# Rotating queries and keys beside their projection, and transposing the latents' tiles between the attention heads

## The chip, the cores and the metric

The kernel runs on one core of one Trainium2 chip. The metric is the device time of one execution in microseconds; the time before is the median of three runs. All arithmetic is in 32-bit floats.

## The reference, cut to what matters

The whole program is a two-layer network with a third block behind it. The change touches only the first mixer of the first layer. It has 512 tokens, 256 of a context and 256 latents, in four tiles of 128 (tiles 0 and 1 are the context, 2 and 3 the latents). What is computed there:

```python
q_m, k_m, v_m, o_m, g_m, q_a, k_a, v_a = _split(h @ w_in, AB_WIDTHS)
outs = [_directional(_mlstm_scan, mc + gc[d], ml + gl[d], init, d == 1) for d in range(2)]
a_lat = _window_attention(_rope(ql, cos, sin), _rope(kl, cos, sin), vl, kc, vc, sink)
a_ctx = _context_attention(qc, kc, vc, sink)
cat = [head_norm(m) * sigmoid(o_m), a];  y = cat @ w_out

def _rope(x, cos, sin):
    x1, x2 = x[..., 0::2], x[..., 1::2]
    return stack([x1 * cos - x2 * sin, x1 * sin + x2 * cos], -1)
```

Attention has 8 query heads of width 64, and 2 key heads, each shared by 4 query heads. Context queries see the 256 context keys; latent queries see these and the latents within 128 positions, so up to 512. Context queries and keys have no positions; the kernel rotates them by an angle of zero (cosine 1, sine 0), so that all four tiles go one way.

## The kernel before, in words

The program is a row of stages. Each stage has its own semaphores and its own program per engine, and ends with a barrier: all engines finish, GpSimd clears the stage's semaphores one by one, and the next stage starts on all of them. So a stage lasts as long as its slowest engine, and nothing of the next one can start earlier, except the weight tiles: `Weights` holds two slots of 2 MB, and whoever frees a slot has SyncE (SP) load the tile that comes after next, also across stages.

The stages around the change:

- **ab_qkv** (`stage_linear`) projects to queries (512 columns), keys (128) and values (128): 768 columns, as one tile of 512 columns and one of 256. For each, TensorE runs 32 products (4 token tiles times 8 slices of the depth), and the four banks are then copied to `qkv`. When a linear stage has no side work (`both`), ScalarE and VectorE copy two banks each; when it has (`side`), ScalarE copies all four (line 215) and VectorE runs the side's parts.
- **mlstm** (`stage_mlstm`), 8 units of matrix products, exponentials and products on VectorE, with one tile of "modulation" in each unit. Its result goes to `hm`.
- **attn** (`stage_attention`). VectorE first rotates one token tile (lines 1266 to 1279) into single buffers `qr` and `kr`; TensorE turns them by five 128x128 transposes (lines 1175, 1176) into the PSUM tile `ps_t`; ScalarE copies them out to `qt` and `kt` (1227, 1228); and so on for four tiles. Then come 32 units, 8 heads for each token tile: 16 context units, numbers 0 to 15, and 16 latent units, 16 to 31. In a step of its loop, for unit u, TensorE multiplies the scores of unit u+2 (1186), transposes the exponentials of unit u+1 (1196) and multiplies the output of unit u (1216). VectorE masks the scores and takes their maximum (1293 to 1300) and scales the output (1312 to 1315); ScalarE takes the exponentials (1242, 1243) and copies the transposed ones (1256).
- Amid these units run four tiles of **modulation** (`Modulation`, lines 413 to 464): a product of a 2 MB weight tile with the conditions (16 short matmul records, 413), a copy to SBUF (430), a product that adds up the parts (422), a sum with the bias (438, 443), and a DMA that stores the row (464). `share` says in which unit a tile runs: tile i in unit i * 32 // 4, that is in units 0, 8, 16 and 24. When a tile's product is done, SP loads the weight tile after next into its slot (113); at the end of the stage SP waits until all rows are stored (469). The modulation's two PSUM banks are those of `ps_t`.
- **ab_norm** (`stage_head_norm`) reads `hm` and writes the first half of `cat`; attention has written the second half. Then `cat` is transposed and projected.

## Time and profile before

| | us |
|---|---|
| median of 3 runs | 3768.81 (3768.76 to 3774.37) |
| the profiled execution, its own time | 3774.25 |
| its span, first to last instruction | 3772.4 |
| TensorE, busy in the span | 3024.5 (80%) |
| VectorE | 1991.3 (53%) |
| ScalarE | 791.2 (21%) |
| GpSimd | 879.9 (23%) |

The two long stretches in the middle of the program are the expert layers, which wait for DMA; the mixer of the change lies at about 60 to 475 us. A line of the timeline gives the start, the duration, the engine, the line of the kernel, what is written and read, how often, and in square brackets how long the engine had been idle and what ended that. PEld is TensorE's loading of weights. The granted clock is 1.00 at 2.4 GHz and 0.50 at 1.2 GHz.

### The profile page before, as it was taken

The numbers are of one execution on the slowest core, as the hardware profiler recorded it, in microseconds if no ns is written. First come the engines' busy times: TensorE is split into PE (matmuls) and PEld (weight loads), VectorE is DVE, ScalarE is ACT, GpSimd is POOL, SyncE is SP. The second block draws the span as 40 slices with busy tenths as digits, with TensorE's granted clock in tenths as the row PEclk, the third lists the DMA queues.
The fourth block names the chain that finished last, engine by engine and source line by source line (L and its number), as shares of the span: only waits on it lengthen the run. The fifth ranks groups of instructions, "written<-read, shape, count | busy, mean of one in ns | idle before, by whom it ended". The sixth has DMA issues, their size and how long they took to land. (4 is left out here: it accounts for less than half of the span.)

```text
span 3772.4 us, 28092 instructions
## 1 busy us (share of the span) xinstructions
PE 3024.5 (80%) x8564; PEld 1486.2 (39%) x8564; DVE 1991.3 (53%) x5057; ACT 791.2 (21%) x2002; POOL 879.9 (23%) x772
## 2 busy tenths in 40 slices
PE   7987788888888888777488667878877597897898
PEld 3444443333333333322243334333332355453663
DVE  1135567777777777776610756767776323223100
ACT  0112312222222222222101312222222130122000
POOL 0000014444444444444100003444444000000000
PEclk9996899999999999999788689999999898898999
DMA  5143229999999999999612247999999343323333
GB/s 195 57 157 112 90 114 427 427 427 427 427 427 423 423 421 417 426 416 427 262 45 91 90 157 322 427 427 427 427 427 427 142 139 116 112 105 130 112 134 122
DMA packets 238156, 1026.04 MB, mean 272 GB/s; under 512 B 41399, under 2 KB 46007, under 8 KB 137639
## 3 DMA queue, kind: packets, MB, share of 16 engines
q0 software_dynamic: 110592, 805.36, 50.8%
q1 hardware_dynamic: 126984, 217.63, 16.5%
q8 instruction: 66, 1.08, 0.1%
q10 hardware_dynamic: 432, 1.31, 0.1%
q14 instruction: 82, 0.66, 0.0%
HBM read 1023.10 MB, written 1.13 MB: 272 GB/s over the span
## 5 line engine op out<-in xcount | busy, mean ns | idle before, releaser
L1528 PE MATMUL l_peer_experts_acc<-l_peer_experts_ring,l_peer_experts_diag 128*128 128x512 f32 x1840 | 860.9, 610 | 217.3 <-ACT l_peer_experts_diag L1567 216.8
L1688 DVE SCALAR_TENSOR_TENSOR l_peer_experts_ring<-l_peer_experts_ring,h_tiles 128x1024 f32<-128x1024 f32 x460 | 563.6, 1225 | 287.4 <-DMA l_peer_experts_ring<-in_expert_rows,l_peer_experts_picks 283.9
L1528 PE MATMUL l_peer_experts_acc<-weight_slots,l_peer_experts_diag 128*128 128x512 f32 x1232 | 581.2, 614 | 150.9 <-ACT l_peer_experts_diag L1567 150.6
L1470 POOL DMA_INDIRECT weight_slots<-in_expert_rows,l_peer_experts_picks x308 | 348.1, 1130 | 1431.1 <-DVE l_peer_experts_picks L1647 1009.0
L1470 POOL DMA_INDIRECT l_peer_experts_ring<-in_expert_rows,l_peer_experts_picks x460 | 531.7, 1156 | 611.5 <-PE l_peer_experts_acc L1528 538.1
L1528 PEld LDWEIGHTS l_peer_experts_acc<-l_peer_experts_ring,l_peer_experts_diag 128*128 128x128 f32 x1840 | 337.4, 192 | 710.9 <-issue 397.3
L1688 DVE SCALAR_TENSOR_TENSOR weight_slots<-weight_slots,h_tiles 128x1024 f32<-128x1024 f32 x308 | 377.4, 1225 | 190.8 <-DMA weight_slots<-in_expert_rows,l_peer_experts_picks 188.3
L1528 PEld LDWEIGHTS l_peer_experts_acc<-weight_slots,l_peer_experts_diag 128*128 128x128 f32 x1232 | 227.9, 194 | 481.7 <-issue 274.7
L1560 ACT ACTIVATE l_peer_experts_gel<-l_peer_experts_dots 128x2 f32<-128x2 f32 x384 | 78.2, 204 | 1207.6 <-DVE l_peer_experts_ring L1688 727.1
L1567 ACT ACTIVATE l_peer_experts_diag<-const_ident,l_peer_experts_wgt 128x128 f32<-128x128 f32 x768 | 266.4, 394 | 225.8 <-DVE l_peer_experts_wgt L1664 209.8
L1495 PE MATMUL l_peer_experts_queries<-h_t,l_query_weights 128*128 128x512 f32 (+3 forms) x576 | 182.0, 461 | 3.9 <-PEq L61 3.9
L1495 PEld LDWEIGHTS l_peer_experts_queries<-h_t,l_query_weights 128*128 128x128 f32 x576 | 106.2, 201 | 76.0 <-issue 67.3
L191 PE MATMUL b_mlp_acc<-weight_slots,b_up 128*128 128x512 f32 x256 | 111.5, 599 | 3.9 <-DVEq L280 3.9
L191 PE MATMUL b_mlp_acc<-b_h_t,weight_slots 128*128 128x256 f32 x512 | 110.8, 379 | 2.5 <-ACTq L266 2.5
L191 PEld LDWEIGHTS b_mlp_acc<-b_h_t,weight_slots 128*128 128x128 f32 x512 | 97.2, 190 | 16.0 <-ACTq L266 2.9
L191 PE MATMUL b_g_acc<-weight_slots,b_h_t 128*128 128x512 f32 x192 | 88.3, 614 | 10.4 <-ACTq L266 10.4
L1664 DVE TENSOR_TENSOR l_peer_experts_wgt<-l_peer_experts_gel,l_peer_experts_scratch 128x2 f32<-128x2 f32 x384 | 60.1, 157 | 52.6 <-ACT l_peer_experts_gel L1560 23.1
L191 PEld LDWEIGHTS b_mlp_acc<-weight_slots,b_up 128*128 128x128 f32 x256 | 49.2, 193 | 65.8 <-issue 65.8
L288 DVE TENSOR_TENSOR b_up<-b_up x8 | 9.8, 1225 | 108.6 <-ACT b_up L215 108.6
L213 DVE COPY b_down<-b_mlp_acc 128x512 f32<-128x512 f32 x2 | 1.4, 692 | 111.9 <-PE b_mlp_acc L191 111.9
L191 PE MATMUL b_xbc_acc<-b_h_t,weight_slots 128*128 128x256 f32 x256 | 58.0, 387 | 2.1 <-ACTq L266 2.1
L191 PE MATMUL b_za_acc<-weight_slots,b_h_t 128*128 128x512 f32 x128 | 57.4, 606 | 2.5 <-ACTq L266 2.5
(464 smaller groups left out, 3367.1 us busy)
## 6 DMA issues: line engine op xcount, KB each, us to landing
weight_slots<-in_w_mod SPq DMA_DIRECT2D x24, 2048.0 KB, 7.8
weight_slots<-in_w_in SPq DMA_DIRECT2D x20, 2048.0 KB, 7.7
l_query_weights<-query_weights SPq DMA_DIRECT2D x16, 1024.0 KB, 9.0
weight_slots<-in_w_mlp_up SPq DMA_DIRECT2D x8, 2048.0 KB, 7.8
weight_slots<-in_w_mlp_down SPq DMA_DIRECT2D x8, 2048.0 KB, 7.7
weight_slots<-in_gla_w_in SPq DMA_DIRECT2D x6, 2048.0 KB, 8.4
weight_slots<-in_ab_w_in SPq DMA_DIRECT2D x5, 2048.0 KB, 8.8
l_ln_rows<-mod_rows SPq DMA_DIRECT2D x16, 512.0 KB, 9.5
```

The source lines that it names most:

```text
L191: last = nc.tensor.matmul(acc[0:rows, half, bank, col:col + cols], lhs, rhs, start=(b == 0 and k == 0), stop=(b == kb - 1 and k == KC - 1))
L213: ins = nc.vector.tensor_copy(dst, src)
L288: nc.vector.tensor_tensor(dst, dst, dst, ALU.mult)
L1470: pool.indirect_dma_start(rows(b, k, None), None, uv, bass.IndirectOffsetOnAxis(ap=picks[:, b % 4, k:k + 1], axis=0)).then_inc(landing(b, ...
L1495: ins = nc.tensor.matmul(q_ps[:, n % 2, 0:hi - lo], wq_slots[:, visit % 2, k, half * P:(half + 1) * P], h_t[:, k, g * n_tok + lo:g * n_tok ...
L1528: ins = nc.tensor.matmul(acc[:, b % 2, c * BANK:(c + 1) * BANK], diag[:, k % DIAGS, :], row[:, c * BANK:(c + 1) * BANK], start=(k == 0), s ...
L1560: nc.scalar.activation(gel[:, b % 2, two], dots[:, b % 2, two], ACT.Gelu).then_inc(gelu_done, 1)
L1567: scaled = nc.scalar.activation(diag[:, k % DIAGS, :], ident, ACT.Copy, scale=wgt[:, b % 2, k:k + 1])
L1664: nc.vector.tensor_tensor(wgt[:, step % 2, two], gel[:, step % 2, two], share[:, step % 2, two], ALU.mult).then_inc(w_ready, 1)
L1688: nc.vector.scalar_tensor_tensor(row, row, 1.0, h[:, tile_of(b), :], ALU.mult, ALU.mult, accum_out=dots[:, b % 2, k:k + 1]).then_inc(dotte ...
```

## The change

Four edits belong together.

1. The rotation leaves attention. `rotation_parts` is handed to ab_qkv as its side work: VectorE rotates the queries of all four tiles once the first column tile (512 columns, the queries) is copied out, and the keys of all four tiles, in one go, once the second is. `qr` and `kr` now hold all four tiles, and to make room `hm` is no longer a tensor of its own: it is the first half of `cat`, and ab_norm works in place.
2. Because ab_qkv now has side work, ScalarE copies all four banks, and VectorE none.
3. In attention only token tiles 0 and 1 are transposed ahead of the units. Tile 2 is transposed in unit 1, tile 3 in unit 3 (TensorE: `turn_in`; ScalarE: `copy_in`).
4. The modulation's tiles run in units 5, 13, 21 and 29 (`shift=5`), since they share the PSUM banks of the transposes.

```diff
+        st.emptied = act_out
         parts = side(st) if side else []
...
-        return [i for i in range(self.tiles) if i * units // self.tiles == u]
+        return [i for i in range(self.tiles) if i * units // self.tiles + self.shift == u]
...
+def rotation_parts(nc, st, qkv, cos, sin, qr, kr):
...
+    def queries(dve):
+        nonlocal links
+        link = Link(dve, chain)
+        dve.wait_ge(st.emptied, 3)
+        for m in range(TT):
+            x = qkv[:, m, 0:A_Q].rearrange("p (h r two) -> p h r two", two=2, r=32)
+            c, s = (w[:, m, :].unsqueeze(1).to_broadcast([P, H_A, 32]) for w in (cos, sin))
+            p1, p2, p3, p4 = products(link, x[:, :, :, 0], x[:, :, :, 1], c, s, None)
...
+    def keys(dve):
+        link = Link(dve, chain, links)
+        dve.wait_ge(st.emptied, 4)
...
+    return [{"vector": queries}, {"vector": keys}]
...
-        mod = Modulation(nc, st, weights, "mod1_first", *mod_args, 0, [ps_t[:, i, :] for i in range(2)])
+        mod = Modulation(nc, st, weights, "mod1_first", *mod_args, 0, [ps_t[:, i, :] for i in range(2)], shift=5)
...
+                turn_in(0)
+                turn_in(1)
+
+                pe.wait_ge(copied, 2)
...
                 for u, (m, kv, j) in enumerate(units):
+                    if u in (1, 3):
+                        turn_in(2 + u // 2)
+                    if u == 5:
+                        pe.wait_ge(copied, TT)
...
+                copy_in(0)
+                copy_in(1)
                 exponentials(0)
                 for u, (m, kv, j) in enumerate(units):
                     b, n = u % 2, keys(m)
+                    if u in (1, 3):
+                        copy_in(2 + u // 2)
                     if u + 1 < len(units):
                         exponentials(u + 1)
...
-        hm = sb("ab_hm", [P, TT, M_W])
+        hm = cat[:, :, 0:M_W]
...
-            stage_linear(nc, "ab_qkv", weights, h_t, tiles, qkv)
+            qr = sb("ab_qr", [P, TT, GROUP, H_KV, DH_A])
+            kr = sb("ab_kr", [P, TT, H_KV, DH_A])
+            stage_linear(nc, "ab_qkv", weights, h_t, tiles, qkv,
+                         side=lambda st: rotation_parts(nc, st, qkv, consts["cos"], consts["sin"], qr, kr))
```

On ScalarE, the copies at the end of ab_qkv, before:

```order
L215 ACTIVATE ab_qkv<-ab_qkv_acc 128x512 [waits ab_qkv_mm_done]
L215 ACTIVATE ab_qkv<-ab_qkv_acc 128x512
L215 ACTIVATE ab_qkv<-ab_qkv_acc 128x256 [waits ab_qkv_mm_done]
L215 ACTIVATE ab_qkv<-ab_qkv_acc 128x256
```

and of the change (ScalarE's copies; then VectorE's first tile of queries and, behind the fourth tile, the keys, where `ab_qkv_rot` are the four buffers of products):

```order
L216 ACTIVATE ab_qkv<-ab_qkv_acc 128x512 [waits ab_qkv_mm_done]
L216 ACTIVATE ab_qkv<-ab_qkv_acc 128x512 x3
L216 ACTIVATE ab_qkv<-ab_qkv_acc 128x256 [waits ab_qkv_mm_done]
L216 ACTIVATE ab_qkv<-ab_qkv_acc 128x256 x3
...
L1137 TENSOR_TENSOR ab_qkv_rot<-ab_qkv,const_cos 128x256 [waits ab_qkv_act_out]
L1138 TENSOR_TENSOR ab_qkv_rot<-ab_qkv,const_sin 128x256
L1139 TENSOR_TENSOR ab_qkv_rot<-ab_qkv,const_sin 128x256
L1140 TENSOR_TENSOR ab_qkv_rot<-ab_qkv,const_cos 128x256
L1155 TENSOR_TENSOR ab_qr<-ab_qkv_rot 128x4x32 [waits ab_qkv_rot_chain]
...
L1167 TENSOR_TENSOR ab_kr<-ab_qkv_rot 128x256 x2
```

VectorE's four copies are gone from this stage, ScalarE has four more, and VectorE has 38 rotation instructions in their place: 32 for the queries and 6 for the keys.

On TensorE, the first units of attention, before (`attn_turn` is the PSUM tile `ps_t`; L413 is a modulation tile):

```order
L1186 MATMUL attn_scores<-attn_kt,attn_qt 128x256 [waits attn_masked]
L1196 MATMUL attn_p_turn<-const_ident,attn_p 128x128 [waits attn_exped]
L1196 MATMUL attn_p_turn<-const_ident,attn_p 128x128
L413 MATMUL attn_turn<-weight_slots,silu_c 32x512 [waits weights_loaded0]
L413 MATMUL attn_turn<-weight_slots,silu_c 32x512 x7
L1216 MATMUL attn_out<-ab_qkv,attn_pt 128x64 [waits attn_p_copied]
L1216 MATMUL attn_out<-ab_qkv,attn_pt 128x64
L422 MATMUL attn_turn<-attn_mod_parts,const_add_up 2x512 [waits attn_mod_parted]
```

and of the change, from the score of unit 2 on:

```order
L1228 MATMUL attn_scores<-attn_kt,attn_qt 128x256 [waits attn_masked]
L1238 MATMUL attn_p_turn<-const_ident,attn_p 128x128 [waits attn_exped]
L1238 MATMUL attn_p_turn<-const_ident,attn_p 128x128
L1262 MATMUL attn_out<-ab_qkv,attn_pt 128x64 [waits attn_p_copied]
L1262 MATMUL attn_out<-ab_qkv,attn_pt 128x64
L1214 MATMUL attn_turn<-const_ident,ab_qr 128x128 [waits attn_copied]
L1214 MATMUL attn_turn<-const_ident,ab_qr 128x128 x3
L1215 MATMUL attn_turn<-const_ident,ab_kr 128x128
L1228 MATMUL attn_scores<-attn_kt,attn_qt 128x256 [waits attn_masked]
L1238 MATMUL attn_p_turn<-const_ident,attn_p 128x128 [waits attn_p_copied,attn_exped]
```

The modulation tile has left unit 0, and unit 1 begins with the five transposes of tile 2.

On TensorE, the end of attention in the change, where unit 29 now holds a modulation tile:

```order
L414 MATMUL attn_turn<-weight_slots,silu_c 32x512 [waits attn_mod_taken,weights_loaded1]
L414 MATMUL attn_turn<-weight_slots,silu_c 32x512 x7
L1262 MATMUL attn_out<-ab_qkv,attn_pt 128x64 [waits attn_out_taken,attn_p_copied]
L1262 MATMUL attn_out<-ab_qkv,attn_pt 128x64 x3
L423 MATMUL attn_turn<-attn_mod_parts,const_add_up 2x512 [waits attn_mod_parted]
L1238 MATMUL attn_p_turn<-const_ident,attn_p 128x128 [waits attn_p_copied,attn_exped]
```

Only two units come behind it, where seven came behind the last tile before.

## Rows read from the trace of the kernel before

**Rows 1.** Busy time, clock and DMA in the attention stage (columns in the first line).

```profile
core 0: us, PE busy (x) PEld busy (x) DVE busy (x) ACT busy (x) POOL busy (x), PEclk, DMA share, GB/s
312.60:434.90 122.30, 101.42 (x444) 58.38 (x444) 81.41 (x274) 44.14 (x136) 0.00 (x0) 0.74 0.20 70
```

**Rows 2.** Timeline: copies out of PSUM in ab_o and ab_qkv, then mlstm's start.

```profile
170.74 2.06 ACT L215 ACTIVATE ab_o<-ab_o_acc 128x512 f32<-128x512 f32 x4 [1.75 <-PE ab_o_acc L191]
...
218.38 0.66 ACT L215 ACTIVATE ab_qkv<-ab_qkv_acc 128x256 f32<-128x256 f32 x2 [12.73 <-PE ab_qkv_acc L191]
218.38 0.76 DVE L213 COPY ab_qkv<-ab_qkv_acc 128x256 f32<-128x256 f32 x2 [12.52 <-PE ab_qkv_acc L191]
...
219.91 1.09 PE L1029 MATMUL mlstm_m_bcast<-ab_m_rows,const_sel 4*128 4x512 f32 x2 [1.57 <-PEq L61]
```

**Rows 3.** Timeline: rotation of the first of four tiles in attention, its transposes.

```profile
312.66 0.49 DVE L1266 TENSOR_TENSOR attn_rot<-ab_qkv,const_cos 128x320 f32<-128x320 f32 x1 [3.17 <-PEq L61]
...
313.88 0.48 DVE L1269 TENSOR_TENSOR attn_rot<-ab_qkv,const_cos 128x320 f32<-128x320 f32 x1
314.39 0.49 DVE L1277 TENSOR_TENSOR attn_qr<-attn_rot 128x128 f32<-128x128 f32 x2
...
315.80 0.47 PE L1175 MATMUL attn_turn<-const_ident,attn_qr 128*128 128x128 f32 x1 [8.22 <-DVEq L1280]
```

**Rows 4.** Timeline: the last tile's transposes, and the first scores.

```profile
325.32 1.12 PE L1175 MATMUL attn_turn<-const_ident,attn_qr 128*128 128x128 f32 x4 [1.84 <-DVEq L1280]
...
327.65 2.07 PE L1186 MATMUL attn_scores<-attn_kt,attn_qt 64*128 64x256 f32 x4 [0.99 <-ACT attn_kt L1228]
```

**Rows 5.** Timeline: the score products that open units 0, 4, 8 and 9.

```profile
331.79 1.22 PE L1186 MATMUL attn_scores<-attn_kt,attn_qt 64*128 64x256 f32 x2
...
344.57 1.22 PE L1186 MATMUL attn_scores<-attn_kt,attn_qt 64*128 64x256 f32 x2
...
354.62 1.22 PE L1186 MATMUL attn_scores<-attn_kt,attn_qt 64*128 64x256 f32 x2
...
361.79 0.70 PE L1186 MATMUL attn_scores<-attn_kt,attn_qt 64*128 64x256 f32 x2
```

**Rows 6.** Timeline: the same products where they open units 12, 15, 16, 17, 19.

```profile
367.84 1.22 PE L1186 MATMUL attn_scores<-attn_kt,attn_qt 64*128 64x256 f32 x2
...
376.23 2.07 PE L1186 MATMUL attn_scores<-attn_kt,attn_qt 64*128 64x512 f32 x2
380.03 2.07 PE L1186 MATMUL attn_scores<-attn_kt,attn_qt 64*128 64x512 f32 x2
...
388.91 1.12 PE L1186 MATMUL attn_scores<-attn_kt,attn_qt 64*128 64x512 f32 x2
...
394.52 1.12 PE L1186 MATMUL attn_scores<-attn_kt,attn_qt 64*128 64x512 f32 x2
```

**Rows 7.** Timeline: modulation in unit 24, the stage's last result, the next stage.

```profile
410.43 1.92 PE L413 MATMUL attn_turn<-weight_slots,silu_c 128*32 128x512 f32 x16
...
432.47 0.28 DVE L1315 TENSOR_SCALAR h_tiles<-attn_out,attn_small 128x64 f32<-128x64 f32 x1 [0.63 <-PE attn_out L1216]
434.91 0.40 ACTq L1334 DMA_DIRECT2D ab_norm_rows<-in_ab_norm_w  x1
```

**Rows 8.** DMA issues between 200 and 440 us, KB and us to landing.

```profile
weight_slots<-in_w_mod SPq DMA_DIRECT2D x12, 2048.0 KB, 7.8
...
attn_sink<-in_ab_sink SPq DMA_DIRECT2D x1, 4.0 KB, 2.5
```

**Rows 9.** Windows: ab_qkv's first products; then units 10 to 13 (columns: rows 1).

```profile
175.00:176.00 1.00, 0.87 (x2) 0.63 (x3) 0.00 (x0) 0.00 (x0) 0.00 (x0) 0.81 0.20 66
...
179.00:180.00 1.00, 1.00 (x4) 0.48 (x3) 0.00 (x0) 0.00 (x0) 0.00 (x0) 0.98 0.00 0
...
364.00:368.00 4.00, 3.02 (x15) 2.31 (x15) 3.47 (x15) 2.33 (x10) 0.00 (x0) 0.85 0.81 313
368.00:372.00 4.00, 4.00 (x13) 2.58 (x14) 2.40 (x9) 1.76 (x7) 0.00 (x0) 0.50 0.00 0
```

More of the change, by code:

```diff
@@ L1124, in stage_mlstm, with products @@
     mod.done()
-def stage_attention(nc, qkv, cos, sin, bars, sink, ident, cat, weights, mod_args):
-    heads = H_A + H_KV
+def rotation_parts(nc, st, qkv, cos, sin, qr, kr):
+    t1, t2, t3, t4 = (st.sb(f"rot{i}", [P, H_A, 32]) for i in range(4))
+    chain, rotated = st.sem("rot_chain"), st.sem("rotated")
+    links = 0
+    def products(link, x1, x2, c, s, shape):
+        parts = [t[:, :, :] if shape is None else t[:, :, :].rearrange("p (m h) r -> p m h r", h=shape) for t in (t1, t2, t3, t4)]
+        nc.vector.tensor_tensor(parts[0], x1, c, ALU.mult)
+        nc.vector.tensor_tensor(parts[1], x2, s, ALU.mult)
+        nc.vector.tensor_tensor(parts[2], x1, s, ALU.mult)
+        link(nc.vector.tensor_tensor(parts[3], x2, c, ALU.mult))
+        return parts
+    def queries(dve):
[6 more added lines that the diff above has]
+            p1, p2, p3, p4 = products(link, x[:, :, :, 0], x[:, :, :, 1], c, s, None)
+            for a, b, op, which in ((p1, p2, ALU.subtract, 0), (p3, p4, ALU.add, 1)):
+                for kv in range(H_KV):
+                    hs = slice(kv * GROUP, (kv + 1) * GROUP)
+                    o = qr[:, m, :, kv, :].rearrange("p j (r two) -> p j r two", two=2)[:, :, :, which]
+                    last = nc.vector.tensor_tensor(o, a[:, hs, :], b[:, hs, :], op)
+                link(last)
+        links = link.n
+    def keys(dve):
+        link = Link(dve, chain, links)
+        dve.wait_ge(st.emptied, 4)
+        x = qkv[:, :, A_Q:A_Q + A_KV].rearrange("p m (h r two) -> p m h r two", two=2, r=32)
+        c, s = (w[:, :, :].unsqueeze(2).to_broadcast([P, TT, H_KV, 32]) for w in (cos, sin))
+        p1, p2, p3, p4 = products(link, x[:, :, :, :, 0], x[:, :, :, :, 1], c, s, H_KV)
+        for a, b, op, which in ((p1, p2, ALU.subtract, 0), (p3, p4, ALU.add, 1)):
+            o = kr[:, :, :, :].rearrange("p m h (r two) -> p m h r two", two=2)[:, :, :, :, which]
+            link(nc.vector.tensor_tensor(o, a, b, op))
+    return [{"vector": queries}, {"vector": keys}]
@@ L1135, in stage_attention @@
+def stage_attention(nc, qkv, qr, kr, bars, sink, ident, cat, weights, mod_args):
     scale = DH_A ** -0.5
     with stage(nc, "attn") as st:
-        qr = st.sb("qr", [P, GROUP, H_KV, DH_A])
-        kr = st.sb("kr", [P, H_KV, DH_A])
-        t1, t2, t3, t4 = (st.sb(f"rot{i}", [P, heads, 32]) for i in range(4))
         qt = st.sb("qt", [P, GROUP, TOK])
@@ L1168, in _, with turn_in @@
             def _(pe):
-                for m in range(TT):
-                    pe.wait_ge(rotated, m + 1)
+                def turn_in(m):
                     if m:
@@ L1174, in _ @@
                     for j in range(GROUP):
[L1175 to L1178 removed]
+                        nc.tensor.transpose(ps_t[:, 0, j * P:(j + 1) * P], qr[:, m, j, :, :].rearrange("p a b -> p (a b)"), ident)
+                    nc.tensor.transpose(ps_t[:, 1, 0:P], kr[:, m, :, :].rearrange("p a b -> p (a b)"), ident).then_inc(turned, 1)
+                turn_in(0)
+                turn_in(1)
+                pe.wait_ge(copied, 2)
                 def score(u):
@@ L1223, in _, with copy_in @@
                 link = Link(act, achain)
-                for m in range(TT):
+                def copy_in(m):
                     act.wait_ge(turned, m + 1)
```

32 lines of the change are left out of this document (5 added, 27 removed).

## The prediction

> **What bounds the kernel now.** I read the busy time by stage first, then the timeline around each edit, then the windows for the granted clock, then SyncE's DMAs. The stages are separated by barriers and the change touches three of them, so the question is what each of the three gains or loses; the expert layers behind them see nothing of it. Attention takes 122.3 us, at a mean granted clock of 0.74 [rows 1]: TensorE is at 1.2 GHz for much of it. Its first 15 us are no attention at all: VectorE rotates, TensorE turns, ScalarE copies. One tile costs 3.17 us: the fourth tile's transposes begin at 325.32, the first's at 315.80, and a third of the difference is 3.17 [rows 3, 4]. TensorE idles there. The first scores begin at 327.65 [rows 4], 15.0 us after the stage's start. After that the units run. At the low clock TensorE sets the pace of the context units: four of them take 354.62 - 344.57 = 10.05, so 2.51 each [rows 5]. For some units after a modulation tile the clock is high: units 9 to 11 take 367.84 - 361.79 = 6.05, about 2.0 each [rows 5, 6]. A context unit with a modulation tile at the low clock takes 361.79 - 354.62 = 7.17 [rows 5].
>
> **1. The projection gets longer.** The keys' tile now has four copies on ScalarE instead of two. Two take 0.66 [rows 2], four about 1.3; four copies of 512 columns took 2.06 in the stage before [rows 2]. VectorE's two ended at 219.14 (218.38 + 0.76), the four will end at about 219.65: +0.5. Then the keys are rotated with nothing to cover them. A product of 320 columns starts 0.41 after the last ((313.88 - 312.66) / 3) and the chained one needs 0.51 [rows 3]; for 256 columns I scale the part beyond the 0.22 of a short one and get 0.34 and 0.44. So 3 x 0.34 + 0.44 = 1.46, and two chained results of 256 columns, 2 x 0.44: 2.34 in all, plus 0.1 to be released. Two more semaphores to clear I put at 0.15. **Sum +3.1** (2.5 to 4).
> The queries cost nothing: per tile 1.46, and four results of 128 columns, which start 0.21 apart [rows 3] and are chained twice, 1.06. Four tiles take 10.1 and start when ScalarE has copied the first column tile, at about 206.8; they end at about 217, while TensorE multiplies until 218.4. The cover has 1.4 us to spare, and 2.7 before the keys want VectorE. Were it gone, each us over would be a us on the stage.
>
> **2. mlstm starts with TensorE colder.** TensorE's gap between the two stages was 1.5 us, 218.4 to 219.91 [rows 2], and becomes 4.6. A gap of 4.4 with little in it precedes ab_qkv (ab_o's products end at 170.7), and there the clock falls to half 0.6 us into the new stage and comes back after 3.4 us [rows 9]. Half speed for 3.4 us costs 1.7 of TensorE's time, and mlstm begins with a row of products that everything waits for. **+1.6** (0 if the clock holds, to 2.5). In mlstm's units the clock dips anyway; I expect no more there. That `hm` lies in `cat` changes addresses, no instruction: 0.
>
> **3. Attention's start gets shorter.** Two tiles are turned instead of four, and no rotation is waited for. From a tile's first transpose to the next thing TensorE can do is 327.65 - 325.32 = 2.33 [rows 4], so scores begin 4.66 after the start instead of 15.0: **-10.3**.
>
> **4. Two tiles are turned amid the units.** This is not only 1.4 us of transposes. In unit 1 ScalarE's next instructions are the copies, ahead of the exponentials that TensorE's next transposes wait for; so a unit is the turn (1.4), the copies (0.9), the exponentials (0.9) and then the rest as before. Against a low-clock unit I count 2.1 more: 4.6 instead of 2.5, twice. At least the transposes' 1.4, at most the whole 2.33 plus a release, 2.6.
>
> **5. The modulation moves, and the clock with it.** From the first scores to unit 0 it is 331.79 - 327.65 = 4.1, as before. Then, with rows 5 and 6 for each kind of unit: unit 0 2.5, units 1 to 4 4.6 + 2.5 + 4.6 + 2.5, unit 5 with modulation 7.2, units 6 to 8 6.05, units 9 to 12 10.0, unit 13 with modulation 7.2. Units 14 to 16 now run right behind a modulation tile, so at the high clock. Two latent units at the high clock take 394.52 - 388.91 = 5.6 [rows 6]; the first behind a modulation tile is short; I put the three at 7.2 (6 to 8.4). Unit 17 then begins 58.5 after the first scores; before it was 388.91 - 327.65 = 61.3, with units 15 at 3.8 and 16, with its modulation, at 8.9 [rows 6]. So **-2.8**, with the turns of part 4 already in it. Unit 17 loses its catch-up: +0.3. Modulation 24 becomes 21, at the same clock: 0.
>
> **6. The last modulation comes late.** Behind unit 24 seven units followed, behind 29 only two. The product takes 1.92 [rows 7] and part of it hides in the last units' waits for ScalarE; walking the last three units through with their durations, the last result comes 1.05 later, at 433.8 in the old time. But SP must see the row stored before the stage can end. In the same old time the product is done at 429.05, a 2 MB weight load is issued there, and the store at about 432.3. A load of that size takes 7.8 to land [rows 8]; if the little store lands with it, that is 436.85. From a stage's last work to the next stage's first instruction it is 0.77 at least (219.91 - 219.14 [rows 2]) and 2.16 here (434.91 less the last result's end at 432.75 [rows 7]), so the next stage would start at 437.6 to 439.0; the engines alone would give 433.8 + 2.16 = 436.0. The wait costs 1.6 to 3.0 more, or 0 to 1.0 if the store takes the 2.5 of a small transfer [rows 8]. I take 2.3, because the store is issued in the middle of the load. The Trainium skill, in DMA: Bandwidth & Descriptors, section Queues, rings and completion order, says that the semaphore write of a transfer lands only after every earlier write from that DMA engine. By that rule the sum is the one I make; by the other price it would be 1.8 us lower. **+1.05 and +2.3.**
>
> **The sum.** Attention: -10.3 - 2.8 + 0.3 + 1.05 + 2.3 = -9.5. With +3.1 and +1.6: **-4.8 us**. The profiled execution took 3774.25 (its span 3772.4), which is at the upper end of the three runs; the sum is a difference, and I take it from the median: 3768.8 - 4.8 = 3764.0. That is 0.13% of the time, and about 0.2%, 7.5 us, is what a measurement of this kernel can tell from no change.
>
> **The rivals.**
> A. **The clock drops as the latents begin.** Units 10 to 13 show it falling some 7 us behind a modulation tile, from 0.85 to 0.50 [rows 9]. What holds it before is the modulation in unit 16, in the thick of the latents. If it falls at unit 16 and stays low to the modulation in 21, five units run at the low clock. Such a unit is the 3.8 of unit 15 [rows 6] plus 0.9 for its longer output, 4.7 instead of 2.8: 5 x 1.9 = 9.5, and 1.0 for modulation 21 at the low clock. -4.8 + 10.5 = +5.7, **3774.5, slower than before**. It decides at unit 16: low clock there and this rival is right. Against it: latent units keep TensorE busier than context units, and once high, the clock stayed: the score product takes 2.07 at 380.03 and 1.12 at 388.91 and 394.52 [rows 6], and modulation 24, 22 us further on, still goes through in 1.92 [rows 7].
> B. **TensorE warms up at once.** With no rotation to wait for, its first 15 us are denser. If the high clock comes by unit 0, the plain units 0, 2, 4 save 0.5 each, the units with turns 1.2 each, modulation 5 some 1.2: -5.1, **3758.9**. The Trainium skill, in TensorE: Matmul & The Clock Gate, Part 1, says that the throttled state is the default and that activity releases it. What speaks against it is that units 4 to 8 kept TensorE at work without a gap for 12 us and the clock stayed low until the modulation's products: the unit at 354.62 still opens with a product of 1.22, that at 361.79 with one of 0.70 [rows 5].
> C. **The turns cost less or the projection's end more than I think**, without a new mechanism: mlstm's start may be warm (-1.6), the store may be quick (-1.8), the keys or the turns may take a microsecond more. This is the forecast's own range, 3760 to 3768.5. That the queries' rotation isn't covered, so that the change doesn't do what it says, would need VectorE 14% slower than its rows show; I give that 3 in 100, inside C.
>
> **How the numbers follow.** Forecast and C 0.74, A 0.13, B 0.13. The range takes in B and C, and most of A, whose price is an upper one, since a later clock rise would cut it: 3758.5 to 3773. Faster by over 7.5 us: most of B, and the low tail of the forecast, 0.2. Slower by over 7.5 us: A with the projection's upper bound, 0.05. Within: 0.75.
>
> **What would show it.** In the changed profile: ab_qkv's last rotation ends at about 222.1 and mlstm starts near 223; VectorE idle between queries and keys; mlstm's first products at clock 0.5; scores 4.7 us after attention's start; units 1 and 3 of 4.6; units 14 to 20 at clock 1.0; SP waiting at attention's end for a row's store. The prediction is wrong if the three stages together, from 174.8 to ab_norm's start, change by anything but -9 to 0 us, or if the stages behind change at all.

## The result, and the profile after

The changed kernel takes 3782.51 us (median of 15 runs), the kernel before, run beside it, 3773.61 us (15 runs). The ratio is 1.0024, with a 95% interval of 1.0017 to 1.0031: **8.9 us slower**. The forecast was 4.8 us faster. The profiled execution took 3777.12 (span 3775.3) against 3774.25.

The stages touched, by the first instruction of each in the two traces (each figure is rounded by itself):

| us | before | after | difference | forecast |
|---|---|---|---|---|
| ab_qkv | 44.8 | 48.6 | +3.8 | +3.1 |
| mlstm | 92.8 | 95.4 | +2.7 | +1.6 |
| attention | 122.3 | 125.0 | +2.7 | -9.5 |
| ab_norm and ab_turn | 22.8 | 22.0 | -0.7 | 0 |
| sum, to ab_out's first product | 282.6 | 291.1 | +8.5 | -4.8 |

The sum is close to the 8.9 us between the medians. What lies behind these stages can't be read that finely from one trace each: from ab_out's first product to the end it is 3314.7 us before and 3310.3 in the changed kernel, and between 3306.5 and 3319.7 in the fourteen traces of this study, none of which edits anything there. With 1.2 us less ahead of these stages, that is why the two profiled executions are only 2.9 us apart. By the prediction's own sign of being wrong, the three stages together changed by +9.2 us, outside -9 to 0. Windows of the changed kernel over the same stages, TensorE alone (columns in the first line):

```profile
core 0: us, PE busy (x), PEclk, DMA share, GB/s
174.00:222.58 48.58, 43.74 (x129) 0.95 0.20 70
222.58:318.00 95.42, 76.24 (x352) 0.86 0.52 186
318.00:442.95 124.95, 110.16 (x444) 0.69 0.19 68
```

Attention runs the same 444 matrix records as before, but they take 110.2 us where they took 101.4, and the mean granted clock is 0.69, not 0.74 [rows 1]. That is the first thing to see: the stage lost its rotation and yet TensorE is busy for longer.

**The projection's end and mlstm's start.** Timeline of the changed kernel:

```profile
217.78 1.21 ACT L216 ACTIVATE ab_qkv<-ab_qkv_acc 128x256 f32<-128x256 f32 x4 [11.75 <-PE ab_qkv_acc L192]
219.10 0.43 DVE L1137 TENSOR_TENSOR ab_qkv_rot<-ab_qkv,const_cos 128x256 f32<-128x256 f32 x1 [2.97 <-ACT ab_qkv L216]
...
220.56 0.89 DVE L1167 TENSOR_TENSOR ab_kr<-ab_qkv_rot 128x256 f32<-128x256 f32 x2
...
222.58 1.73 PE L1030 MATMUL mlstm_m_bcast<-ab_m_rows,const_sel 4*128 4x512 f32 x2 [4.84 <-PEq L61]
224.24 6.41 PE L1021 MATMUL mlstm_scores<-y_tiles 128*128 128x512 f32 x8
```

Four copies in 1.21 us, the keys rotated from 219.10 to 221.45, the next stage 1.1 us later. VectorE was idle for 2.97 before the keys, so the queries' rotation was covered. TensorE was idle for 4.84 us where it had been 1.57 [rows 2], and its first row of score products takes 6.41 us.

**Attention.** The first scores begin at 322.64, 4.6 us after the stage's start. The turn of tile 2, in unit 1:

```profile
329.15 1.06 PE L1214 MATMUL attn_turn<-const_ident,ab_qr 128*128 128x128 f32 x4
330.00 0.42 PE L1215 MATMUL attn_turn<-const_ident,ab_kr 128*128 128x128 f32 x1
...
332.09 0.69 PE L1238 MATMUL attn_p_turn<-const_ident,attn_p 128*128 128x128 f32 x2 [0.52 <-ACT attn_p L1290]
...
333.45 1.22 PE L1228 MATMUL attn_scores<-attn_kt,attn_qt 64*128 64x256 f32 x2
```

The unit takes 4.3 us. So far it goes as forecast. Now the same engine as the latents begin (units 15 to 20), then the modulation in unit 21:

```profile
374.03 1.12 PE L1228 MATMUL attn_scores<-attn_kt,attn_qt 64*128 64x512 f32 x2
376.31 0.98 PE L1238 MATMUL attn_p_turn<-const_ident,attn_p 128*128 128x128 f32 x4 [1.16 <-ACT attn_p L1290]
377.08 0.95 PE L1262 MATMUL attn_out<-ab_qkv,attn_pt 128*128 128x64 f32 x4
377.96 2.07 PE L1228 MATMUL attn_scores<-attn_kt,attn_qt 64*128 64x512 f32 x2
...
396.56 2.07 PE L1228 MATMUL attn_scores<-attn_kt,attn_qt 64*128 64x512 f32 x2
...
401.21 2.07 PE L1228 MATMUL attn_scores<-attn_kt,attn_qt 64*128 64x512 f32 x2
...
404.26 3.37 PE L414 MATMUL attn_turn<-weight_slots,silu_c 128*32 128x512 f32 x16
```

The score product doubles from 1.12 to 2.07 between 374.03 and 377.96 and stays there. From 377.96 to 401.21 there are five units, 16 to 20, of 4.65 us; before, two latent units at the high clock took 5.6 together [rows 6]. The granted clock in windows of the changed kernel:

```profile
222.00:223.00 1.00, 0.42 (x1) 0.95 1.04 408
223.00:224.00 1.00, 1.00 (x2) 0.50 1.06 412
...
370.00:376.00 6.00, 4.91 (x23) 1.00 0.75 259
377.00:407.00 30.00, 30.00 (x98) 0.50 0.01 5
407.00:441.00 34.00, 28.39 (x168) 1.00 0.35 125
```

The low level, 1.2 GHz, holds from 376.5 to 407.2. In the kernel before it ended at 387.2, behind the modulation tile in unit 16. A TensorE busy for 30.00 of 30.00 us is no sign of health here: it is busy because it is slow.

**Attention's end.** Timeline of the changed kernel, then SyncE's waits between 430 and 444 us (us in all, times, the longest):

```profile
433.05 0.39 SPq L113 DMA_DIRECT2D weight_slots<-in_ab_w_out  x1
...
436.16 0.23 SPq L465 DMA_DIRECT2D mod_rows<-attn_mod_rows  x1
...
437.46 0.28 DVE L1345 TENSOR_SCALAR h_tiles<-attn_out,attn_small 128x64 f32<-128x64 f32 x1 [0.40 <-PE attn_out L1262]
442.94 0.40 ACTq L1364 DMA_DIRECT2D ab_norm_rows<-in_ab_norm_w  x1
```

```profile
SPq L470 <- DMA mod_rows<-attn_mod_rows: 4.3, 1, 4.3
```

From the last result's end (437.74) to the next stage it is 5.2 us, where it was 2.16 [rows 7]: 3.0 more. The store of 4 KB, issued at 436.16, is waited for until 440.7; the last of the 2 MB load issued ahead of it lands at 440.9.

So two suspects are large (the clock in the latents, the colder mlstm) and two are of the forecast's size (the projection, the store). Theory 1: the change moved the modulation tiles, and with the tile that left unit 16 went the latents' high clock. The rivals: the clock falls at the latents whatever is put there, and the loss is in the turns, in the projection, or in `hm` being a part of `cat`.

### The profile page after: what moved, and what is told of

The parts are those of the page before. It is cut to its first block and busy times, and to the rows that moved or that the text cites. A ratio compares the mean times of both kernels' runs of the same rounds, so it can differ in the third digit from the quotient of the medians.

```text
span 3775.3 us, 28084 instructions
## 1 busy us (share of the span) xinstructions
PE 3030.5 (80%) x8564; PEld 1490.6 (39%) x8564; DVE 1989.5 (53%) x5051; ACT 792.3 (21%) x2006; POOL 882.4 (23%) x772
## 5 line engine op out<-in xcount | busy, mean ns | idle before, releaser
L192 PE MATMUL b_g_acc<-weight_slots,b_h_t 128*128 128x512 f32 x192 | 88.3, 614 | 10.4 <-ACTq L267 10.4
```

What stands on the lines that cost most here:

```text
L192: last = nc.tensor.matmul(acc[0:rows, half, bank, col:col + cols], lhs, rhs, start=(b == 0 and k == 0), stop=(b == kb - 1 and k == KC - 1))
```

## The experiments

All ratios are to the kernel before, run on the same chip; 0.0001 is 0.38 us. Stage lengths are from one profiled execution each, by the first instruction of each stage.

| kernel | median, us | ratio (95%) | ab_qkv | mlstm | attention |
|---|---|---|---|---|---|
| before | | 1 | 44.8 | 92.8 | 122.3 |
| changed | 3782.51 | 1.0024 (1.0017 to 1.0031) | 48.6 | 95.4 | 125.0 |
| 1 tiles in 5, 8, 16, 24 | 3769.26 | 0.9992 (0.9983 to 1.0000) | 48.1 | 95.7 | 114.1 |
| 2 before, tiles shifted | 3782.48 | 1.0026 (1.0017 to 1.0035) | 44.8 | 90.8 | 131.6 |
| 3 store first | 3778.95 | 1.0016 (1.0007 to 1.0025) | 48.0 | 96.2 | 121.6 |
| 4 products beside the keys | 3775.19 | 1.0007 (0.9998 to 1.0015) | 48.0 | 90.5 | 125.3 |
| 5 third tile in 16 | 3773.45 | 1.0001 (0.9992 to 1.0010) | 48.6 | 95.8 | 114.9 |
| 6 all turned ahead | 3771.12 | 1.0001 (0.9992 to 1.0010) | 48.6 | 95.7 | 116.2 |
| 7 = 1 + 4 | 3764.81 | 0.9984 (0.9976 to 0.9993) | 48.0 | 92.4 | 114.1 |
| 8 = 7, third in 14 | 3779.48 | 1.0020 (1.0009 to 1.0031) | 48.1 | 90.9 | 126.8 |
| 9 products in 16 | 3769.80 | 0.9994 (0.9985 to 1.0004) | 48.6 | 95.5 | 117.6 |
| 10 = 7 + products at mlstm's end | 3762.57 | 0.9976 (0.9967 to 0.9985) | 48.0 | 92.5 | 113.4 |
| 11 = 7, third in 15 | 3765.27 | 0.9982 (0.9973 to 0.9991) | 48.0 | 92.3 | 112.2 |
| 12 one product in 15 | 3770.76 | 0.9995 (0.9986 to 1.0004) | 48.1 | 93.1 | 113.0 |

### 1. The tiles back in their old places

```diff
-            return [i for i in range(self.tiles) if i * units // self.tiles + self.shift == u]
+            return [i for i in range(self.tiles) if self.at[i] == u]
...
+        mod.at = [5, 8, 16, 24]
```

> The changed kernel with attention's modulation tiles in units 5, 8, 16 and 24 (so all but the first where they were before the change). Theory 1, the places of the modulation tiles set the clock of the latents: a tile in unit 16 raises the clock for units 17 to 20, which took 4.65 us each in the changed kernel and then take about 2.8, and with the last tile in unit 24 SyncE has no store to wait for at the end (3.0 us there, and 1.0 for the last product). Attention falls from 124.9 to 112 to 115 us, the whole by 10 to 12 us, to 1 to 3 us below the kernel before. Rival, the clock falls as the latents begin whatever is put there, or the turns amid the units are what costs: attention stays at 120 or more, and only the 3 to 4 us at its end go.

Measured: 0.9992 against 1.0024, so 12.1 us faster than the changed kernel, and attention took 114.1. Windows of this kernel:

```profile
364.00:383.80 19.80, 19.80 (x60) 0.50 0.06 24
384.20:428.00 43.80, 39.30 (x221) 1.00 0.28 97
```

The clock comes up at 384.0, behind the tile in unit 16, and stays to the end. Theory 1 holds; the turns amid the units are still in this kernel, so they are not the loss.

### 2. The kernel before, with the shift alone

```diff
-        mod = Modulation(nc, st, weights, "mod1_first", *mod_args, 0, [ps_t[:, i, :] for i in range(2)])
+        mod = Modulation(nc, st, weights, "mod1_first", *mod_args, 0, [ps_t[:, i, :] for i in range(2)], shift=5)
```

> The kernel before with one part of the change alone: its four modulation tiles in attention go to units 5, 13, 21 and 29. Theory 1: the latents lose the clock between units 15 and 20 (about 7 us more) and the last store is waited for (4 us with the last product), so this is 9 to 13 us slower than before, attention about 133 us. Rival, the slowdown of the changed kernel comes from the longer projection, the colder mlstm and the turns, and the tiles' places are worth only their store: 3 to 4 us slower, attention at 126.

Measured: 1.0026, 9.8 us slower than before, and attention took 131.6, 9.3 more. The window of the low clock in this kernel:

```profile
379.00:409.00 30.00, 30.00 (x94) 0.50 0.00 1
```

One number in the source (`shift=5`), without any rotation moved, costs as much as the whole change. The two experiments are each other's converse, and they agree. Note mlstm: 90.8 here and 92.8 in the kernel before, with the same instructions. So two us of that stage can differ between two executions without an edit to it, and single traces can't be read finer than that.

### 3. The last row is stored ahead of the load

```diff
             sp.wait_ge(self.multiplied, i + 1)
-            self.weights.load(sp, i + 2)
+            if not late:
+                self.weights.load(sp, i + 2)
...
             sp.dma_start(self.mod_rows[:, at:at + BANK], self.rows[:, i % 2, :]).then_inc(self.stored[i % 2], 16)
+            if late:
+                self.weights.load(sp, i + 2)
```

Here `late` is true for the last tile of attention.

> The changed kernel with one order changed on SyncE: the last tile's row is stored before the next weight load is issued, not behind it. In the changed kernel the store went out at 436.16 and was waited for until about 442.2, with a 2 MB load issued at 433.05. If the load is what holds the store up, the store lands 2.5 to 3 us after it is issued, the next stage starts 2.5 to 3 us earlier, and the whole is 2.5 to 3 us faster than the changed kernel, unless the later load is missed behind (it was issued 3 us later). If a store takes its time whatever goes beside it, nothing changes.

Timeline of this kernel:

```profile
436.43 0.23 SPq L467 DMA_DIRECT2D mod_rows<-attn_mod_rows  x1
...
436.70 0.39 SPq L113 DMA_DIRECT2D weight_slots<-in_ab_w_out  x1
...
440.03 0.40 ACTq L1368 DMA_DIRECT2D ab_norm_rows<-in_ab_norm_w  x1
```

The next stage starts 3.60 us after the store is issued; it was 6.78 in the changed kernel. Attention is 3.4 shorter. The ratio says 3.0 us less, which by itself is within its uncertainty of some 4 us; the trace decides. The store landed 1.2 us after it was issued, where in the changed kernel it took 4.5 and landed with the load (at 440.7, not the 442.2 of the expectation), and from the last result's end to the next stage it is 2.1 us again, as it was before the change. So the store had waited for the load. The Trainium skill, in DMA: Bandwidth & Descriptors, section Queues, rings and completion order, has the rule that gives this, that a transfer's semaphore write lands only after the earlier writes of the same DMA engine; these two kernels agree with it.

### 4. Products beside the keys' rotation

```diff
+    def keep_warm(pe):
+        pe.wait_ge(st.emptied, 3)
+        for i in range(4):
+            nc.tensor.matmul(st.acc[:, 0, i % 4, :], st.act_t[:, 0, 0:P], st.act_t[:, 1, 0:BANK], start=True, stop=True)
+    return [{"vector": queries}, {"vector": keys}] + [{}] * 6 + [{"tensor": keep_warm}]
```

> The changed kernel with four products of 512 columns more on TensorE, whose results nobody reads, into emptied accumulators while the keys are rotated at ab_qkv's end (1 us or so of the 4.6 in which TensorE idled). If mlstm's 2.7 us more came from a clock that fell in that gap (0.95, then 0.50 from 223 on, 6.41 us for the first eight score products against 3.70), the clock holds longer and mlstm gives back 1.5 to 2.7 us. If it came from something else (the place of mlstm's output, which now lies in another tensor, or its own end, where a store is waited for), mlstm stays at 95.4.

They ran for 3.60 us, from 220.40, not the 1 us of the expectation. mlstm's first score products in this kernel:

```profile
226.42 3.70 PE L1022 MATMUL mlstm_scores<-y_tiles 128*128 128x512 f32 x8
```

3.70 instead of 6.41, and mlstm took 90.5. In the six traces of the changed projection without these products (changed, 1, 3, 5, 6, 9) mlstm took 95.4 to 96.2, and 93.1 in number 12; in the five with them (4, 7, 8, 10, 11) 90.5 to 92.5; in the two with the old projection 90.8 and 92.8. `hm` lies in `cat` in all but the last two, so it costs nothing. What goes with the length of mlstm is the time that it spends at the low clock: 16 us of it in the traces with 90.5 to 90.9, 17 to 22 us in those with 92.3 to 93.1, 27 to 28 us in those with 95.4 to 96.2. The stretch at its start, 6.8 us of it in mlstm in the changed kernel, is the part of this that the products took away (in number 11 they left 3.4); the short ones in its middle fall differently from trace to trace, and number 12, with the stretch at the start and one less in the middle, took 93.1. By the ratios the products are worth 6.4 us here and 3.0 us from number 1 to number 7; each of these differences is uncertain by some 4 to 5 us, and mlstm in the traces says 4.9 and 3.3.

### 5. Only the third tile moved

```diff
+        mod.at = [5, 13, 16, 29]
```

> The changed kernel with one modulation tile of attention moved: the third, from unit 21 to unit 16; the others stay in 5, 13 and 29. If it is the tile in unit 16 that gives the latents their high clock, the low stretch (376.6 to 407.2 in the changed kernel, 30.7 us) ends after unit 16, some 18 us earlier, the four units 17 to 20 take 2.8 instead of 4.65, and the whole is 6 to 8 us faster than the changed kernel: 3775 to 3776.5, 1.5 to 3 us above the kernel before, with the store's wait at the end still there. Rival: the gain of the kernel with tiles in 5, 8, 16 and 24 came from its end (no store to wait for) and from the tile in unit 8. Then this one stays within 2 us of the changed kernel.

Measured: 8.7 us faster than the changed kernel by the ratios, attention 114.9. The low stretch behind unit 14 lasted 6.8 us, from 377.2 to 384.0, instead of 30.7. Most of number 1's gain is this one tile.

### 6. The change without its second half

```diff
-                turn_in(0)
-                turn_in(1)
-
-                pe.wait_ge(copied, 2)
+                for m in range(TT):
+                    turn_in(m)
+
+                pe.wait_ge(copied, TT)
...
-                copy_in(0)
-                copy_in(1)
+                for m in range(TT):
+                    copy_in(m)
...
+        mod.at = [0, 8, 16, 24]
```

> The rotation stays in the projection, but attention turns all four tiles ahead of its heads and the modulation tiles are in units 0, 8, 16 and 24 as before the change. So this is the change without its second half. By the theory of the terms: projection 3.3 to 4 us longer, mlstm 2 to 3 us longer (both as in the changed kernel), attention's first scores 4 turns of 2.33 us = 9.3 after its start instead of 15.0, so 5.7 us shorter; 0 to 1.5 us slower than before in all, 3 to 5 us slower than the kernel with two tiles turned amid the units and tiles in 5, 8, 16 and 24. Rival: the turns amid the units cost all that they save at the start, and this one is as fast as that, or faster.

Timeline of this kernel:

```profile
319.86 1.08 PE L1218 MATMUL attn_turn<-const_ident,ab_qr 128*128 128x128 f32 x4 [6.21 <-PEq L61]
...
329.13 2.07 PE L1232 MATMUL attn_scores<-attn_kt,attn_qt 64*128 64x256 f32 x4 [1.00 <-ACT attn_kt L1275]
```

Scores begin 9.3 us after the start, as worked out. The ratio is 1.0001, 3.4 us above number 1, at the low end of what was expected, and attention took 116.2 against 114.1. Two turns amid the units seem to save 2 to 3 us net of what they cost there. This speaks against the rival, but 3.4 us between two ratios is uncertain by more than that, and the first modulation tile moved too (unit 0 for unit 5), so it isn't shown.

### 7. Both repairs

> The changed kernel with tiles in 5, 8, 16 and 24 and with the four products on TensorE while the keys are rotated. The first edit alone took 13.3 us off the changed kernel, the second 7.3 (medians). If the two repairs are independent, this one is at 3761 to 3763.5, 0.3% faster than before. If the second one's gain was partly the chance of a clock phase (mlstm took 95.4 in the changed kernel and 91 with the products; in the trace of the kernel before with shifted tiles the same mlstm was 2 us shorter than before without an edit to it), only 3 to 5 us are added: 3764 to 3766.

Measured: 0.9984, 6.0 us faster than before. The second repair added 3.0 us by the ratios and 3.3 by mlstm in the traces. That is what the rival said; with an uncertainty of 4 to 5 us the ratios alone would not rule out the 7.3 of a full sum.

### 8. The third tile in unit 14

```diff
-        mod.at = [5, 8, 16, 24]
+        mod.at = [5, 8, 14, 24]
```

> As the last, but with the third modulation tile in unit 14 instead of 16. The question is what lets the clock stay up. In the changed kernel a tile in unit 13 raised the clock at 369.7 and it fell again at 376.6, as the latents began. If any latent unit at the high clock keeps it there, a tile in unit 14 gives a warm start to the latents, units 15 and 16 too, and this is 2 to 4 us faster than with 16. If the clock falls some 7 us behind a tile whatever follows in that stretch, and only a tile amid the latents holds it, units 17 to 23 run at the low clock and this is 8 to 13 us slower than with 16.

Timeline, then the window of the low clock, both of this kernel:

```profile
381.35 0.66 PE L1248 MATMUL attn_p_turn<-const_ident,attn_p 128*128 128x128 f32 x4 [0.94 <-ACT attn_p L1300]
381.84 1.09 PE L1272 MATMUL attn_out<-ab_qkv,attn_pt 128*128 128x64 f32 x8
382.87 2.07 PE L1238 MATMUL attn_scores<-attn_kt,attn_qt 64*128 64x512 f32 x2
```

```profile
383.00:420.00 37.00, 37.00 (x112) 0.50 0.00 1
```

The clock rose at 376.1, ran through the scores of the first two latent units and fell at 382.9: 37.6 us at the low level, 14.7 us in the medians. The twelve executions are in two groups: eleven took 3776.7 to 3783.5 us, with a mean granted clock of 0.924 to 0.928, and one took 3762.47, as fast as number 7, with 0.932. So the same kernel can keep the clock here or lose it; with the tile in unit 14 it nearly always lost it.

### 9. Products in place of a tile

```diff
                     mod.tensor(pe, u, len(units))
+                    if u == 16:
+                        pe.wait_ge(mod.taken, 1)
+                        for i in range(3):
+                            nc.tensor.matmul(ps_t[:, 0, :], qt[:, 0, 0:P], qt[:, 0, :], start=True, stop=True)
```

> The changed kernel, its modulation tiles left in 5, 13, 21 and 29, and in unit 16 three products of 128 by 512 more on TensorE, whose results nobody reads; no DMA, no VectorE and no ScalarE work comes with them. They cost 5.1 us at the low clock (six records of 0.85), about as much of TensorE as a modulation tile (3.6 us and its 1.0). Theory: what a tile in unit 16 gives the latents is TensorE's work alone, so the low stretch (376.6 to 407.2) ends behind unit 16, some 18 us earlier, and the four units 17 to 20 give back 7.4 and the tile in unit 21 1.3: 3 to 4 us faster than the changed kernel net of the products. Rival: it is something else of the tile (its 2 MB load, VectorE's part), or the clock rises by the latents' own count of units; then the low stretch ends where it did and this is 5 us slower than the changed kernel.

Timeline, then windows of this kernel:

```profile
381.48 3.96 PE L1258 MATMUL attn_turn<-attn_qt 128*128 128x512 f32 x6
```

```profile
377.00:383.80 6.80, 6.80 (x17) 0.51 0.18 67
384.00:434.00 50.00, 43.78 (x250) 1.00 0.24 85
```

The clock comes up while they run. 4 us of work that nobody needs made attention 7.4 us shorter and the kernel 11.3 us faster than the changed one by the ratios, more than the 3 to 4 expected: the slow units and the tile in 21 had cost 12.0 (number 12), not the 8.7 that I had counted, and the products ended at the high clock, 4.0 us instead of 5.1. So TensorE's work is enough to raise the clock, without the load and the VectorE work that come with a tile.

### 10. Products behind mlstm's last one

```diff
                     mod.tensor_sums(pe, u, n_units)
+                for i in range(5):
+                    nc.tensor.matmul(ps_s[:, i % TT, :], qk_t[:, H_M, 0:P], qk_t[:, 0, :], start=True, stop=True)
```

> The kernel with tiles in 5, 8, 16 and 24 and four products at ab_qkv's end, and now five products more behind mlstm's last one, in the 7 us in which TensorE idles until attention's first transposes (311.13 + 1.02 to 318.0 in the changed kernel). They end before the stage does, so they cost nothing. If the low clock of attention's first 34 us comes from that idle time, the clock holds longer into attention, the first turns and units run at 2.0 for 2.5 us, and it is 2 to 5 us faster than without the products. If the turns and the context's units let the clock fall by themselves, only the first one or two slices of attention are faster: 0 to 1.5 us.

Windows of this kernel:

```profile
315.30:318.70 3.40, 1.50 (x10) 1.00 0.05 4
319.00:342.00 23.00, 20.52 (x68) 0.50 0.01 1
```

The products ended 1.74 us before attention's first transpose. Two turns run at the high clock, then it falls; attention took 113.4 against 114.1. So the context's start does not hold the clock even when it begins at the high level. This version is at 0.9976, **9.1 us faster than before and 18 faster than the changed kernel**, the best of the study; what it gains over number 7 (3.0 us) is within the uncertainty.

### 11. The third tile in unit 15

> As the kernel with the third tile in unit 14, but in unit 15. With 14 the clock fell again at 382.8, 6.8 us behind its rise at 376.0, in eleven of twelve executions by their times, and the kernel was 14.7 us slower than with 16. Scores and transposes of the latents are begun one and two units ahead, so behind unit 15 there is more latent work than behind 14. If the clock's hold depends on what TensorE does in the first 7 us behind the rise, 15 holds it (all of that is latent work) and is 0 to 2 us faster than 16, or holds it in a part of the executions, which then fall into two groups some 15 us apart. If only 16 or later holds, 15 is as slow as 14.

Timeline, then the window behind the rise, both of this kernel:

```profile
383.32 0.66 PE L1248 MATMUL attn_p_turn<-const_ident,attn_p 128*128 128x128 f32 x4 [0.49 <-ACT attn_p L1300]
```

```profile
378.00:428.00 50.00, 42.26 (x237) 1.00 0.24 85
```

By their times (3762.7 to 3769.7, the same as number 7) it held in all eleven executions. So the border lies between units 14 and 15.

### 12. One product in the wait

```diff
+                    if u == 15:
+                        pe.wait_ge(mod.taken, 1)
+                        for i in range(1):
+                            nc.tensor.matmul(ps_t[:, 0, :], qt[:, 0, 0:P], qt[:, 0, :], start=True, stop=True)
                     if u + 1 < len(units):
                         turn(u + 1)
```

> The changed kernel, its modulation tiles left in 5, 13, 21 and 29, and one product of 128 by 512 more on TensorE in unit 15, between that unit's score product and the transposes of the first latent unit. There TensorE waited 1.16 us for ScalarE (374.03 + 1.12 to 376.31) just before the clock fell at 376.6; in the kernel with the third tile in 14 it waited 0.94 just before the fall, in the two in which the clock held (third tile in 15 and 16) no wait behind the rise was longer than 0.49. The product takes 0.9, so it costs nothing. If that wait is what lets the clock fall, it now holds from 369.8 on, the low stretch of 30.7 us is gone, units 15 to 20 take 2.8 instead of 4.65 and the tile in unit 21 1.92 instead of 3.37: 11 to 13 us faster than the changed kernel, 2 to 4 us faster than before. If the clock falls there whatever fills the wait, nothing changes.

Timeline of this kernel in unit 15, at the tile in unit 21, and two windows:

```profile
375.57 1.12 PE L1228 MATMUL attn_scores<-attn_kt,attn_qt 64*128 64x512 f32 x2
376.63 1.12 PE L1255 MATMUL attn_turn<-attn_qt 128*128 128x512 f32 x2
377.86 0.66 PE L1238 MATMUL attn_p_turn<-const_ident,attn_p 128*128 128x128 f32 x4
...
394.74 1.92 PE L414 MATMUL attn_turn<-weight_slots,silu_c 128*32 128x512 f32 x16
```

```profile
355.50:372.00 16.50, 16.50 (x59) 0.50 0.02 6
372.50:430.00 57.50, 50.75 (x277) 1.00 0.31 111
```

This is the changed kernel with its tiles where the change put them and one product more. The low stretch of 30.7 us is gone: the clock stays high from 372.3 to 430.3, the tile in unit 21 takes 1.92 instead of 3.37, and attention 113.0 instead of 125.0. By the ratios it is 10.9 us faster than the changed kernel; against the kernel before, its interval does not exclude 1. One product of 1.12 us at the border of context and latents, where TensorE had stood still for ScalarE for 1.16 us, is enough to keep the clock. The Trainium skill, in TensorE: Matmul & The Clock Gate, section A second HAM failure mode: psum-queue depth-cycling, describes a kernel that idles only briefly between groups of products, often enough for the clock to swing. This case is like it in that the idle time is short, but here one wait, not many, came before the fall.

Whether it was the wait that let the clock fall is not shown. The product did two things: it filled the wait, and it gave TensorE work of the kind that lifted the clock in number 9. No run put the product at another place nearby, or closed the wait without a product. And a wait of this size does not bring the clock down by itself. A window of the changed kernel in mlstm, and a line of its timeline there:

```profile
301.00:315.00 14.00, 9.09 (x64) 0.99 0.79 282
```

```profile
306.85 1.92 PE L414 MATMUL mlstm_mod<-weight_slots,silu_c 128*32 128x512 f32 x16 [2.06 <-DVE mlstm_mod_rows L439]
```

TensorE waited 2.06 us and the clock stayed high for 8 us more, with a modulation tile right behind the wait; it stayed high over a wait of 1.61 us that ended at 275.89 too. In the context units of the same kernel it fell at 356.0 after waits of no more than 0.84. So what TensorE does around a wait counts as well as its length.

## Why the prediction was wrong

The forecast failed at one step, **part 5, "Units 14 to 16 now run right behind a modulation tile, so at the high clock"**, and at what it took for granted behind them, units 17 to 20. Against the sum of -4.8 the traces give +8.5, 13.3 apart:

- **Part 5, the clock in the latents: +12.0.** Units 14 to 16, put down at 7.2 us, took 10.4 (372.21 to 382.61), and units 17 to 20 took 18.6, where two latent units at the high clock take 5.6 [rows 6]. Number 12, the changed kernel with one product more and without the low stretch, has attention at 113.0 us, 12.0 less; 122.3 less the forecast's 9.5 is 112.8. So all other terms of attention together were right to 0.2 us, in part because two of them missed in opposite ways (the turns and the store, below), and the whole of its error is the low stretch. Rival A named the mechanism, its cause (the tile that leaves unit 16) and a price, 10.5 for five units and the tile in 21. Five whole units, 16 to 20, did run at the low clock; unit 21 took 8.3 us (401.21 to 409.54) where unit 24 of the kernel before, with its tile at the high clock, took 6.0, so 2.3 more instead of 1.0; and the clock fell within unit 15. I gave it 0.13. The argument against it was "once high, the clock stayed", drawn from units 17 to 23 of the kernel before. Those come after the border; units 10 to 13, which showed a fall behind a tile, were the nearer rows. And with a tile in unit 13 the rise falls right at the border, where TensorE waits for ScalarE's first latent exponentials. The trace of before could not show that wait at the high clock, because there the border was crossed at the low clock; the range should have held both ends.
- **Part 1, the projection: +3.8 for +3.1.** The copies (1.21), the keys (2.35) and the queries under cover (10.06) were as worked out, though the prediction doesn't spell out the scaling that gives 0.34 and 0.44 (the trace has 0.34 and 0.45); from TensorE's last product to the next stage it is 4.84 instead of 1.57, so +3.3. The other 0.6 is the clock at the projection's own start, low for 6.8 us in this trace and for 3.4 in eight of the twelve with the new projection: in those the stage took 48.0 to 48.1, so +3.2.
- **Part 2, the colder mlstm: +2.7 for +1.6.** The mechanism was right: the low stretch is from 222.9 to 229.7, twice the 3.4 us taken from [rows 9], and in number 4, without it, mlstm took 4.9 us less. The size lies above my upper bound of 2.5, by less than one trace can tell.
- **Part 3: -10.3**, right: the first scores came 4.6 us after the start. **Part 4: 4.3 us per unit with a turn, for 4.6**, right in kind; units 0 to 3 together took 13.4 (326.77 to 340.13) for the 14.2 put down, so a turn costs 1.7 more, not 2.1.
- **Part 6: +3.0 for +2.3.** The store landed with the load, as chosen, and the next stage began 2.3 us later. Number 3 gave the 3 us back.
- Behind attention 0.7 was gained, since ab_turn's transposes, 5.70 us instead of 6.53, ran partly at the high clock; I had put 0.

12.0 for the low stretch, 0.2 for the rest of attention, 0.7 and 1.1 for parts 1 and 2, less 0.7 behind attention: 13.3 of 13.3. Each of these is a difference of two single traces, so that it closes so well is luck.

Rival B, TensorE warming at once, did not come: the clock was low from 315.1 to 349.2, until the tile in unit 5. Even when attention began at the high clock it fell after 3.6 us (number 10).

Two faults stand behind the step. I priced the clock by which kind of unit is at work, as if "a latent unit keeps it" were a property of the unit; the runs show the same latent units at either clock, and that one product of about a microsecond at the right place decides between them. And the chances were set by how much argument each case had, not by how near its rows were.

## What to carry to other kernels

When small TensorE jobs (modulation tiles, side products) are moved among the units of a stage that runs near the clock's edge, read the granted clock along the stage first, and ask which of these jobs lifts it and what wait comes next behind each. A filler product of 1.12 us in the wait ahead of the fall was worth 11 us here, and four beside an exposed stretch of VectorE's work 3 to 6. A stage's last store belongs ahead of the next big weight load on its queue, or far enough from the stage's end.

## What the runs showed of the hardware

- A wait of TensorE of 1.16 us (changed kernel) or 0.94 us (number 8) preceded a fall of the granted clock to 0.50, and with a product in its place the clock held (number 12); in the latents it held over waits of 0.49 (number 11). But length alone does not decide: in mlstm of the changed kernel the clock held over waits of 1.61 and 2.06 us, and in its context units it fell after waits of 0.84 and 0.26.
- At 0.50 the latents kept TensorE busy for 30.00 of 30.00 us (changed kernel), and the clock did not come up; a modulation tile or three plain products in unit 16 brought it up. Why these raise it and the latents' own unbroken products do not stays open: no run here varied the kind of product.
- The same program can hold or lose the clock from one execution to the next: in number 8 eleven of twelve executions have a mean granted clock of 0.924 to 0.928, and the twelfth, at least 14 us faster, 0.932. Number 12 has two groups too, five executions of 3765.5 to 3767.6 and six of 3770.8 to 3772.6; what parts them was not traced, since only one was profiled.
- A 4 KB store issued 3.1 us behind a 2 MB load on one queue landed 4.5 us later, with the load; issued ahead of the load it landed in 1.2 (number 3).
